# Rotary lanes moved by a VectorE shuffle instead of a TensorE product, and waits by column in a two-block fp32 layer

## The chip, the cores and the metric

One Trainium2 chip; the program runs on one of its cores. The metric is the device time of one execution in microseconds (us), median of the runs. All arithmetic is fp32. PE is TensorE, DVE VectorE, ACT ScalarE, POOL GpSimd, and SP the queue that issues the weight loads.

## What is computed

Two blocks for 256 tokens of width 1024. The first is a gated linear attention (GLA) with latent attention (MLA) beside it, an output product, a mixture of experts and a gated embedding:

```python
x = x + merged @ w_out[layer]
hm = rmsnorm(x, ln_moe[layer]).reshape(B * S, D)
x = x + hierarchical_moe(hm, ...)          # top-1 group of 8, then top-2 experts in it, 64 experts in all
ple_gate = jax.nn.sigmoid(rmsnorm(x, ln_ple[layer]) @ w_ple_gate[layer])
x = x + (p[layer] @ w_ple_proj[layer]) * ple_gate
```

The second is a modulated attention and convolution block; its queries and keys get a rotary embedding over rows and columns of a grid:

```python
def _rot_half_axial(u):
    u1, u2, u3, u4 = jnp.split(u, 4, axis=-1)          # head of 64: quarters of 16
    return jnp.concatenate([-u2, u1, -u4, u3], axis=-1)

def _apply_rope(u, cos, sin):
    return u * cos[None, :, None, :] + _rot_half_axial(u) * sin[None, :, None, :]

q = _apply_rope(_heads(parts[4]), cos, sin)
k = _apply_rope(_heads(parts[5]), cos, sin)
y_b = (silu(z_b) * attn) @ w_out_attn
y = (sigmoid(g_a) * y_a + sigmoid(g_b) * y_b) @ w_o
x = x + gt * rmsnorm(y, post_g)
```

## The kernel before

Each engine has one hand-written instruction stream, and semaphores tie the streams together. The order of the work is the order in which the streams are written.

**Weights.** SP streams weights in fills of 1 MB into a ring of 8 slots (`stream_a`, later line 535). A fill is issued once the product that used the slot has ended. In the experts' rounds 4 slots beside the ring join it, and a load waits for the count `moe_used`, which PE raises as it ends with the weights (lines 488 and 492 are the waits, seen in the trace as the line of the issue).

**Products.** A result is 256 output columns for all 256 tokens, in one PSUM bank. `product` (lines 555 to 573) runs two parts of 8 steps k over the width, 16 matmuls. With `feature` (L567) the weights are the stationary operand, without it (L570) the activations are. The profile records each fp32 matmul twice, so one product is 32 records. Banks 0 to 3 serve in turn (`bank_no`), banks 4 to 7 hold transposes and scores. Before the first matmul `product` waits for the bank and for the fill; whether the whole activation operand is there, the caller asks ahead of it.

**The operands.** `turn_rows` (L583) transposes an activation tile into banks 4 to 7. DVE (`turned`, L1524 or L1526) and ACT (L1045) copy the columns k into SBUF with a gain. For "ple" they take four columns each, for "two" (the operand of the second block's products) DVE takes all eight.

**The stages**, in PE's order: input products, modulation, MLA beside the gates, the GLA levels (L727, each masked into place by L1702, `diag` last), GLA values (L747), transposes (L753, L764) copied by ACT (L1200, L1210), products yb, ya, out, first context keys (kc) with router and ranks (L785 to L801), four embedding products (pp, L570), the gather of the first round (L826), and the expert rounds: up (L847), turn of the hidden rows (L874), down (L886), scatter (L919), whose four banks DVE adds to the residual X (L1868). Five context products (L859, L862) lie in rounds 1 and 2. Then ple, vc (last context values), the products zb, ga, gb, za, b, c, xin, q2, k2, v2, the attention (L981 to L1014), yattn, and last `wo` (L1027) in banks 0 to 7, followed by gain, squares, norm, residual and store.

**Rotation.** ACT copies each result of q2 and k2 to RAW (L1327). One product later PE multiplies RAW by the constant matrix `rot` (L959), into bank 4 or 5. DVE multiplies that bank by the sine (L1933) and RAW by the cosine (L1936), and adds (L1939, L1941). Between two rotations DVE does a quarter-step of the convolution (L1918 to L1923).

**Tail.** For each quarter of `wo`, DVE first writes the gained copy (L1992), then ACT squares the bank (L1359), DVE sums (L1997, L1998), POOL takes the power (L1489), DVE scales and adds X (L2005), SP stores (L540).

```python
pe.wait_ge(S("twoT"), 8)                              # before zb: all eight columns
pe.wait_ge(S("merged2"), 4)                           # before wo: all four pairs
act.wait_ge(S("y_gain"), 4 * t + n + 1)               # ACT's square behind DVE's gain
```

## Time and profile before

| | |
|---|---|
| runs before, us | 1294.29, 1291.46, 1290.39 |
| median | 1291.46 |
| profiled execution, its own time | 1288.38 |
| its span, first to last instruction | 1286.2 |
| PE busy | 1203.9 us, 94% of the span |
| DVE busy | 305.7 us, 24% |
| ACT busy | 211.1 us, 16% |
| POOL busy | 109.2 us, 8% |
| HBM traffic | 321.77 MB read, 251 GB/s over the span |

The profiled execution took 2.2 us more than its span, for what lies around the instructions. The 94% of PE say which engine is loaded, and they count as busy also the time in which its clock was lower. Where a stage waits has to be read from that stage.

### The profile page before, as it was taken

How to read it: one execution, taken by the hardware profiler on the slowest of the kernel's cores; microseconds unless marked ns; L12 is line 12 of the kernel's file. 1: busy time of each engine (PE TensorE's matmuls, PEld its weight loads, DVE VectorE, ACT ScalarE, POOL GpSimd, SP SyncE). 2: the span in 40 equal slices, each digit the busy share in tenths (PEclk: the TensorE clock that was granted, in tenths of full speed). 3: DMA queues.
4: the chain of work that ended last, by engine and by line, in shares of the span. 5: the costliest groups of instructions: out<-in, count | busy, mean ns of one | idle time of the engine just before them, and what ended most of it. 6: DMA issues, size and time to landing. Idle time of an engine off the chain costs nothing.

```text
span 1286.2 us, 14655 instructions
## 1 busy us (share of the span) xinstructions
PE 1203.9 (94%) x6053; PEld 833.1 (65%) x6053; DVE 305.7 (24%) x653; ACT 211.1 (16%) x433; POOL 109.2 (8%) x118
## 2 busy tenths in 40 slices
PE   6999998999999999998888889899999999999998
PEld 5887887887344445433232323788888888876687
DVE  1145348313111111110101010220001014526512
ACT  1232554103000000000000000210000000035501
POOL 0015045001000000000000000000000000125300
PEclk9999999999999999999999999899999999999999
DMA  9799322283699999999999999734444444443300
GB/s 320 258 291 325 124 77 93 76 360 135 271 406 411 411 411 416 415 419 416 420 416 420 416 418 384 231 120 164 144 150 164 146 149 138 151 144 124 99 1 33
DMA packets 149631, 323.60 MB, mean 252 GB/s; under 512 B 8671, under 2 KB 111562, under 8 KB 133194
## 3 DMA queue, kind: packets, MB, share of 16 engines
q1 hardware_dynamic: 143648, 315.33, 65.4%
q0 software_dynamic: 1536, 4.20, 1.2%
q10 hardware_dynamic: 4394, 3.31, 0.8%
q8 instruction: 40, 0.66, 0.2%
q14 instruction: 13, 0.11, 0.0%
HBM read 321.77 MB, written 1.05 MB: 251 GB/s over the span
## 4 chain that ended last, share of the span: by engine, by line
PE 82%; DMA 9%; ACT 2%; issue 2%; DVE 2%; SPq 1%; POOL 1%; ACTq 0%; DVEq 0%; POOLq 0%
PE bank L567 33%; PE bank L847 14%; PE bank L570 12%; DMA AR<-in_w 9%; PE bank L886 6%; PE bank L826 2%; PE bank L859 2%; PE bank L994 1%; PE bank L981 1%; PE bank L862 1%; PE bank L1027 1%; PE bank L1014 1%; PE bank L727 1%; PE bank L919 1%; PE bank L621 1%
## 5 line engine op out<-in xcount | busy, mean ns | idle before, releaser
L567 PE MATMUL bank<-HT,ring 128*128 128x256 f32 x1760 | 386.7, 380 | 3.0 <-DVE HT L1526 2.5
L567 PEld LDWEIGHTS bank<-HT,ring 128*128 128x128 f32 x1760 | 334.2, 191 | 51.2 <-issue 2.9
L847 PE MATMUL bank<-ring,AR 128*64 128x512 f32 x640 | 174.9, 606 | 20.0 <-DMA AR<-in_w 13.1
L847 PEld LDWEIGHTS bank<-ring,AR 128*64 128x64 f32 x640 | 55.4, 139 | 122.4 <-issue 121.8
L847 PE MATMUL bank<-AR 128*64 128x512 f32 x384 | 116.6, 605 | 2.4 <-DMA AR<-in_w 1.5
L886 PE MATMUL bank<-ring,AR 128*64 128x512 f32 x384 | 87.7, 598 | 11.4 <-ACT AR L1256 11.4
L570 PE MATMUL bank<-ring,HT 128*128 128x256 f32 (+1 forms) x384 | 81.9, 373 | 1.0 <-issue 1.0
L1853 DVE TENSOR_TENSOR AR<-AR,bank 128x256 f32<-128x256 f32 x32 | 13.5, 421 | 284.5 <-ACT AR L1247 283.7
L570 PEld LDWEIGHTS bank<-ring,HT 128*128 128x128 f32 x384 | 71.0, 190 | 11.1 <-issue 2.3
L570 PE MATMUL bank<-ring,AR 128*128 128x256 f32 x328 | 73.4, 386 | 3.4 <-DVE AR L1575 1.4
L1388 POOL TENSOR_TENSOR SM<-SM 128x2 f32<-128x2 f32 (+3 forms) x8 | 11.6, 1448 | 708.4 <-DVE SM L1506 658.2
L570 PEld LDWEIGHTS bank<-ring,AR 128*128 128x128 f32 x328 | 63.1, 194 | 13.0 <-DVE AR L1575 1.6
L1247 ACT ACTIVATE AR<-bank 128x256 f32<-128x256 f32 x32 | 12.3, 384 | 348.8 <-PE bank L847 348.8
L886 PEld LDWEIGHTS bank<-ring,AR 128*64 128x64 f32 x384 | 25.5, 136 | 58.1 <-issue 41.1
L847 PEld LDWEIGHTS bank<-AR 128*64 128x64 f32 x384 | 35.5, 139 | 40.0 <-issue 35.1
L567 PE MATMUL bank<-AR,ring 128*128 128x256 f32 x256 | 57.9, 383 | 1.0 <-ACT AR L1210 0.7
L567 PEld LDWEIGHTS bank<-AR,ring 128*128 128x128 f32 x256 | 47.8, 190 | 13.7 <-issue 6.1
L1868 DVE TENSOR_TENSOR X<-X,bank 128x512 f32<-128x512 f32 x32 | 19.8, 682 | 97.6 <-PE bank L919 97.6
L1566 DVE TENSOR_TENSOR AR<-AR,bank 128x512 f32<-128x512 f32 x12 | 8.2, 687 | 131.0 <-ACT AR L1317 80.1
L826 PEld LDWEIGHTS bank<-AR,HN 128*128 128x128 f32 x288 | 33.0, 192 | 6.3 <-issue 4.9
L826 PE MATMUL bank<-AR,HN 128*128 128x64 f32 x288 | 33.8, 276 | 1.0 <-ACT AR L1228 1.0
L886 PE MATMUL bank<-AR 128*64 128x512 f32 x128 | 29.2, 599 | 3.8 <-ACT AR L1256 3.8
(325 smaller groups left out, 1024.7 us busy)
## 6 DMA issues: line engine op xcount, KB each, us to landing
ring<-in_w SPq DMA_DIRECT2D x128, 1024.0 KB, 17.2
AR<-in_w SPq DMA_DIRECT2D x64, 1024.0 KB, 17.8
ring<-in_w_in SPq DMA_DIRECT2D x62, 1024.0 KB, 5.2
ring<-in_w_mod SPq DMA_DIRECT2D x12, 1024.0 KB, 5.9
AR<-in_w_in SPq DMA_DIRECT2D x5, 1024.0 KB, 17.0
ring<-in_w_out SPq DMA_DIRECT2D x4, 1024.0 KB, 5.1
ring<-in_w_ple_gate SPq DMA_DIRECT2D x4, 1024.0 KB, 9.5
ring<-in_w_out_conv SPq DMA_DIRECT2D x4, 1024.0 KB, 5.1
```

Of the source, the lines that this page charges most:

```text
L567: mm = pe.matmul(bank[:, part * T:part * T + T], w[:, k, c0 + part * P:c0 + part * P + P], act[:, k, :], start=(k == 0), stop=(k == k_n - 1))
L570: mm = pe.matmul(bank[:, part * 256:part * 256 + n], act[:, k, part * P:part * P + P], w[:, k, c0:c0 + n], start=(k == 0), stop=(k == k_n ...
L621: mm = pe.matmul(bank_of(i)[32 * g:32 * g + 32, 0:256], CC[:, k, :], w[:, k, :], start=(k < 4), stop=(k >= 4))
L727: mm = pe.matmul(bank[:, h * P:h * P + P], k[:, h, st * P:st * P + P], q[:, h, tt * P:tt * P + P], start=True, stop=True)
L826: mm = pe.matmul(B[0][:, k * SLOT:k * SLOT + SLOT], HN[:, t, k * P:k * P + P], SEL[:, t, 0:SLOT], start=(t == 0), stop=(t == TT - 1))
L847: mm = pe.matmul(bank[e * SLOT:e * SLOT + SLOT, :].rearrange("p (w n) -> p w n", w=2), XG[:, k, :], w, start=(k == 0), stop=(k == DK - 1))
L859: mm = pe.matmul(bank[:, part * T:part * T + T], w[:, k, part * P:part * P + P], HT[:, k, :], start=(k == 0), stop=(k == DK - 1))
L862: mm = pe.matmul(bank[:, part * 256:part * 256 + 256], HT[:, k, part * P:part * P + P], w[:, k, :], start=(k == 0), stop=(k == DK - 1))
L886: mm = pe.matmul(B[5][half * SLOT:half * SLOT + SLOT, :], HHT[:, p % 2, c, e * SLOT:e * SLOT + SLOT], w[:, c, half * 512:half * 512 + 512] ...
L919: mm = pe.matmul(B[SCATTER[2 * t + half]][:, :], STR[rows, t * P:t * P + P], YY[rows, :], start=True, stop=True)
L1853: V_.tensor_tensor(SGM[:, p % 2], SGM[:, p % 2], bank[:, 0:FE], ALU.mult).then_inc(S("moe_silu"), 1)
L1868: ins = V_.tensor_tensor(xs, xs, B[(0, 1, 2, 5)[2 * t + half]][:, :], ALU.add)
```

## The change

1. **Rotation.** The matmul with `rot` goes, and the matrix with it (128 of 1701 constant columns). DVE does a `stream_shuffle` of RAW within each group of 32 lanes, lane to (lane + 16) mod 32, then multiplies by a sine table that has the sign in it.
2. **Column waits.** `product` gets `ahead`, a wait before each k of the first part. It is used in the first product of yb, ya, out, ple, zb and yattn, and `wo` has the same. The producers raise their semaphores per column or pair. The `diag` level of GLA signals each half by itself.
3. **"two" operand.** Its columns 4 to 7 move from DVE to ACT.
4. **Around the first round.** Two steps k of kc run before the transposes of X. The fourth pp product moves behind the gather (banks 0, 1, 3, 2), and DVE computes the expert weights after the first selection of rows.
5. **Residual.** Scatter banks are (0, 1, 5, 2), DVE adds by half of the width, and the transposes after the last round start when the first half is in.
6. **Last product.** yattn uses banks 2, 3, 1, 0 and `wo` banks 4 to 7 first. ACT squares each bank before DVE writes the gained copy, and the norm of a row tile comes before its fourth gain.

```diff
-            def product(i, act, first=None, parts=(0, 1)):
+            def product(i, act, first=None, parts=(0, 1), ks=None, ahead=None):
...
                 for part in parts:
-                    for k in range(k_n):
+                    for k in ks or range(k_n):
+                        if ahead is not None and part == parts[0]:
+                            ahead(k)
...
+            def pairs_of(sem, base=0):
+                return lambda k: pe.wait_ge(S(sem), base + k // 2 + 1) if k % 2 == 0 else None
+            def two_engines(first, second):
+                return lambda k: pe.wait_ge(S(first if k < 4 else second), k % 4 + 1)
...
-            pe.wait_ge(S("gla_a"), len(LEVELS))
             for tt in range(TT):
+                pe.wait_ge(S("gla_a"), len(LEVELS) + tt)
...
-            products("yb", OTM)
+            products("yb", OTM, ahead=pairs_of("omT"))
...
-            products("ya", OTG)
+            products("ya", OTG, ahead=pairs_of("ogT"))
             turn_context(3, B[7])
-            pe.wait_ge(S("merged"), 4)
-            products("out", GATE[:, 0:8, :])
+            products("out", GATE[:, 0:8, :], ahead=pairs_of("merged"))
+            pe.wait_ge(S("cT"), 8)
+            product(of["kc"][0], HT, parts=(0,), ks=range(2))
             pe.wait_ge(S("emptied_dve"), emptied[of["out"][-1]][1])
-            pe.wait_ge(S("cT"), 8)
             turn_rows(lambda k, t: X[:, t, :].rearrange("p (q k) -> p k q", k=DK)[:, k, :])
-            product(of["kc"][0], HT, parts=(0,))
+            product(of["kc"][0], HT, parts=(0,), ks=range(2, DK))
...
             gather()
+            product(of["pp"][-1], PTR)
+            wait_emptied(of["pp"][2])
             moe_round(FIRST, first=True)
...
-            pe.wait_ge(S("moe_x"), rounds + 0)
-            turn_rows(cols(X))
-            pe.wait_ge(S("pleT_dve"), 4)
-            pe.wait_ge(S("pleT_act"), 4)
+            pe.wait_ge(S("moe_x"), rounds * 2)
+            turn_rows(cols(X), halfway=lambda: pe.wait_ge(S("moe_x"), rounds * 2 + 1))
             for i in of["ple"]:
-                product(i, PLT, first=True)
+                product(i, PLT, first=True, ahead=two_engines("pleT_dve", "pleT_act") if i == of["ple"][0] else None)
...
-            pe.wait_ge(S("twoT"), 8)
+            products("zb", HT, ahead=two_engines("twoT", "twoT_act"))
...
-                pe.matmul(B[4 + m % 2][:, :], const("rot"), RAW[:, m % 2, :], start=True, stop=True)\
-                  .then_inc(S("rot_ps"), 1)
...
-            pe.wait_ge(S("na_o"), H2 // 2)
-            products("yattn", HT)
-            pe.wait_ge(S("merged2"), 4)
+            products("yattn", HT, ahead=lambda k: pe.wait_ge(S("na_o"), k + 1))
...
+                        if t == n == 0:
+                            pairs_of("merged2")(k)
-                        mm = pe.matmul(B[4 * t + n][:, 0:256], GA[:, k, t * P:t * P + P], slot_view(f)[:, k, :],
+                        mm = pe.matmul(B[4 - 4 * t + n][:, 0:256], GA[:, k, t * P:t * P + P], slot_view(f)[:, k, :],
...
-                dve.wait_ge(S("rot_ps"), m + 1)
+                dve.wait_ge(S("emptied_act"), emptied[i][1])
                 d3 = dst.rearrange("p (a t) -> p a t", a=2)
-                V_.tensor_tensor(d3, B[4 + m % 2][:, :].rearrange("p (a t) -> p a t", a=2),
-                                 over(const("sinT").unsqueeze(1), 2, T), ALU.mult)
+                link(V_.stream_shuffle(dst, RAW[:, m % 2, :], [(lane + 16) % 32 for lane in range(32)]))
+                V_.tensor_tensor(d3, d3, over(const("sinT").unsqueeze(1), 2, T), ALU.mult)
...
-                    act.wait_ge(S("y_gain"), 4 * t + n + 1)
+                    act.wait_ge(S("wo_ps"), 4 * t + n + 1)
...
-                dve.wait_ge(S("wo_ps"), 4 * t + n + 1)
+                dve.wait_ge(S("y_sq"), 4 * t + n + 1)
```

How the streams move at three places. Lines of the changed file are 9 to 20 higher there: L576 and L579 are the two matmuls of `product`, L846 the gather, L867 the up product, L1036 the matmul of `wo`.

On PE, the last key products before:

```order
L959 MATMUL bank5<-AR,CST 128x512 [waits roped,emptied_act]
L567 MATMUL bank1<-HT,ring 128x256 [waits arr_a5,emptied_act]
L567 MATMUL bank1<-HT,ring 128x256 x15
L959 MATMUL bank4<-AR,CST 128x512 [waits roped,emptied_act]
L570 MATMUL bank2<-ring,HT 128x256 [waits arr_a6,emptied_act]
L570 MATMUL bank2<-ring,HT 128x256 x15
```

and now:

```order
L576 MATMUL bank1<-HT,ring 128x256 [waits arr_a5,emptied_act]
L576 MATMUL bank1<-HT,ring 128x256 x15
L579 MATMUL bank2<-ring,HT 128x256 [waits arr_a6,emptied_act]
L579 MATMUL bank2<-ring,HT 128x256 x15
L579 MATMUL bank3<-ring,HT 128x256 [waits arr_a7,emptied_act]
```

The rotation's matmul is gone from between the products, and no wait on `roped` is left there.

On DVE, one rotation (the first of the queries) as it is now, where the first row stands in place of nothing and the second took bank 4 before:

```order
L1949 STREAM_SHUFFLE AR<-AR 128x512 [waits emptied_act]
L1950 TENSOR_TENSOR AR<-AR,CST 128x512 [waits dve_chain]
L1952 TENSOR_TENSOR AR<-AR,CST 128x512
L1957 TENSOR_TENSOR AR<-AR 128x512 [waits dve_chain]
L1958 TENSOR_SCALAR AR<-AR 128x512 [waits dve_chain]
```

One instruction more for each of eight rotations; it waits for ACT's copy, no longer for PE.

On PE, from the third embedding product (pp) to the first expert product (up) before:

```order
L570 MATMUL bank2<-ring,AR 128x256 [waits emptied_dve]
L570 MATMUL bank2<-ring,AR 128x256 x3
L570 MATMUL bank3<-ring,AR 128x256 [waits emptied_act]
L570 MATMUL bank3<-ring,AR 128x256 x3
L826 MATMUL bank0<-AR,HN 128x64 [waits emptied_act,normed,sel]
L826 MATMUL bank0<-AR,HN 128x64 x15
L847 MATMUL bank3<-AR 64x512 [waits arr_m2,arr_m1,arr_m3,arr_m0,gath]
```

and now:

```order
L579 MATMUL bank3<-ring,AR 128x256 [waits emptied_act]
L579 MATMUL bank3<-ring,AR 128x256 x3
L846 MATMUL bank0<-AR,HN 128x64 [waits emptied_act,sel,normed]
L846 MATMUL bank0<-AR,HN 128x64 x15
L579 MATMUL bank2<-ring,AR 128x256 [waits emptied_dve]
L579 MATMUL bank2<-ring,AR 128x256 x3
L867 MATMUL bank3<-AR 64x512 [waits arr_m1,arr_m2,arr_m0,arr_m3,gath,emptied_act]
```

The last pp product stands between the gather and the product that needs what is gathered.

## Rows read from the trace of the kernel before

**Rows 1.** The page, the span in 40 slices: HBM traffic.
```profile
GB/s 320 258 291 325 124 77 93 76 360 135 271 406 411 411 411 416 415 419 416 420 416 420 416 418 384 231 120 164 144 150 164 146 149 138 151 144 124 99 1 33
```

**Rows 2.** Who PE waited for: line, releaser, us in total, times, longest.
```profile
PE bank L583 <- DVE X L1868: 2.6, 1, 2.6
PE bank L567 <- DVE HT L1526: 2.5, 1, 2.5
...
PE bank L1027 <- DVE AR L1989: 1.5, 1, 1.5
...
PE bank L747 <- DVE AR L1702: 1.4, 1, 1.4
...
PE bank L570 <- DVE AR L1753: 1.1, 1, 1.1
PE bank L826 <- ACT AR L1228: 1.0, 1, 1.0
...
PE bank L570 <- DVE AR L1524: 1.0, 1, 1.0
PE bank L847 <- DVE AR L1834: 0.8, 1, 0.8
PE bank L583 <- DVE X L1757: 0.8, 1, 0.8
...
PE bank L567 <- ACT AR L1210: 0.7, 1, 0.7
...
PE bank L567 <- DVE HT L1967: 0.5, 1, 0.5
PE bank L567 <- ACT AR L1200: 0.3, 1, 0.3
```

**Rows 3.** Windows (us, PE, PEld, DVE, ACT, POOL busy, PEclk, DMA share, GB/s) around the first rounds.
```profile
320.00:330.00 10.00, 10.00 (x50) 3.62 (x48) 1.62 (x6) 0.72 (x2) 0.00 (x0) 1.00 0.25 91
...
400.00:790.00 390.00, 354.64 (x1702) 151.64 (x1700) 45.82 (x110) 26.49 (x66) 0.00 (x0) 0.99 1.02 416
```

**Rows 4.** SP's issues (start, us, count), first round.
```profile
333.71 1.97 SPq L492 DMA_DIRECT2D ring<-in_w  x4
```

**Rows 5.** Timeline of the last GLA masks and of ACT's second operand copy.
```profile
224.74 1.32 DVE L1702 COPY_PREDICATED AR<-MSK,bank 128x512 f32<-128x512 uint8 x2 [0.45 <-PE bank L727]
...
247.00 1.09 ACT L1210 ACTIVATE AR<-bank 128x512 f32<-128x512 f32 x2 [12.27 <-PE bank L764]
```

**Rows 6.** Timeline after the last round: DVE's four columns of the "ple" operand.
```profile
809.18 1.65 DVE L1524 TENSOR_SCALAR AR<-bank,VEC 128x256 f32<-128x256 f32 x4
```

**Rows 7.** Windows after two idle times of PE, columns as in rows 3.
```profile
807.27:814.10 6.83, 5.85 (x22) 4.94 (x21) 1.73 (x5) 3.48 (x8) 0.69 (x1) 0.51 1.10 348
858.60:862.10 3.50, 3.50 (x9) 2.79 (x10) 0.00 (x0) 0.00 (x0) 0.00 (x0) 0.51 0.03 10
```

**Rows 8.** Timeline, DVE's eight columns of the "two" operand.
```profile
854.81 3.71 DVE L1526 TENSOR_SCALAR HT<-bank,SM 128x256 f32<-128x256 f32 x8 [8.40 <-PE bank L583]
```

**Rows 9.** Chain of work in order of time (start, us), rotation stage.
```profile
1075.49 0.86 PE bank L959 x2
1076.35 6.91 PE bank L567 x32
```

**Rows 10.** Windows of one query product with its rotation, and of three v2 products.
```profile
1075.33:1083.10 7.77, 7.77 (x36) 6.46 (x35) 4.12 (x8) 0.60 (x1) 0.00 (x0) 1.00 0.42 137
...
1122.98:1143.70 20.72, 20.68 (x96) 17.86 (x94) 2.63 (x3) 1.19 (x2) 2.12 (x3) 1.00 0.52 161
```

**Rows 11.** Timeline, one instruction on 128 x 512: product with sine, scaling.
```profile
1076.39 0.69 DVE L1933 TENSOR_TENSOR AR<-bank,CST 128x512 f32<-128x512 f32 x1 [3.47 <-PE bank L959]
...
1078.44 0.43 DVE L1942 TENSOR_SCALAR AR<-AR 128x512 f32<-128x512 f32 x1
```

**Rows 12.** Timeline, the tail after the last matmul.
```profile
1280.25 0.43 DVE L1992 TENSOR_TENSOR AR<-bank,PG 128x256 f32<-128x256 f32 x1 [3.03 <-PE bank L1027]
1280.71 0.38 ACT L1359 ACTIVATE HN<-bank 128x256 f32<-128x256 f32 x1 [2.98 <-DVE AR L1992]
```

More of the change, by code:

```diff
@@ L79, in constants @@
     put("ones", 1.0)
-    rot = np.zeros((P, P))
-    for r in range(P):
-        if (r % 32) < 16:
-            rot[r + 16, r] = -1.0
-        else:
-            rot[r - 16, r] = 1.0
-    put("rot", rot)
     half = HD // 2
@@ L802, in _ @@
             pe.wait_ge(S("pT"), 1)
-            products("pp", PTR)
+            for i in of["pp"][:-1]:
+                product(i, PTR)
             FIRST = 0
```

135 lines of the change are left out of this document (70 added, 65 removed).

## The prediction

> **What bounds the kernel now.** I read the span in slices first, then PE's waits, then the timeline around each wait that the change touches. PE is busy for 94% of the span, so the kernel is a chain of PE work, with one stretch of another kind. From the 12th to the 24th of the 40 slices (32.2 us each, so 354 to 772 us) HBM traffic stands at 406 to 420 GB/s [rows 1], and the window from 400 to 790 us shows the DMA engines full all the time while PE is busy for 355 of 390 us [rows 3]. There the experts' weights set the pace. Outside it a microsecond that PE waits or works is a microsecond of the end.
>
> Does a gain before the rounds reach the end, across a stretch bound by DMA? From 320 to 330 us the DMA engines are used at 0.25 [rows 3], so they start with no backlog. The burst that fills them is issued at 333.7 us, when PE has ended the second up product and freed its slots [rows 4]. An earlier PE therefore starts the full stretch earlier, with the same bytes behind it. I take it that the whole stretch moves by what is saved before it.
>
> **The change part by part.** First the waits before the rounds, each a line of [rows 2].
>
> GLA values (L747) wait 1.4 us for the last masks. The two masks start at 224.7 us, held until both halves of the scores are there, and take 0.66 us each [rows 5]. Now the first starts 0.4 us earlier, behind the mask of the level before, and PE starts after it instead of after the second: 0.4 + 0.66 = **1.1**. The second half of the values lies behind the first half's 16 records, longer than a mask, and waits for nothing. yb waits 0.3 for both copies and needs one: **0.3**. ya waits 0.7; its two copies take 1.09 [rows 5], so one of them, **0.5**, goes. out waits 1.1 for the fourth merged pair. Six steps k before it are 12 records of 0.216 us (6.91 by 32 [rows 9]), 2.6 us of cover: **1.1**. The transposes of X wait 0.8 for the residual. Four records of kc, 0.86 us, now lie in that gap, and 2.6 us of kc are left behind the transposes, which is still more than the 1.65 that DVE takes for four columns of such an operand [rows 6]: **0.7**. At the first round PE waits 1.0 before the gather for the last pp bank, and 0.8 before the up product for the gathered rows. The fourth pp product, 8 records or 1.7 us, now covers the second wait, and the first has lost its cause. The expert weights leave DVE's path to the selection: **1.8**. Sum before the rounds: **5.5**.
>
> In the rounds the scatter banks change places and DVE adds in another order. The next round's first use of these banks lies behind an up product. If that cover were lost, each round would show its adds, up to the 2.6 us that PE waits for them after the last one [rows 2], but nothing in the change takes it away: 0.
>
> After the last round the transposes wait 2.6 for the residual [rows 2]. They can start half an addition stage sooner, about 1.2 us, but ACT's squares still need all of X, and DVE's columns stand behind them. So I count nothing for that. The first ple product waits until all four DVE columns are there. These take 1.65 us [rows 6], and now one column suffices, 0.4 us: **1.2**.
>
> At the operand "two" DVE does eight columns in 3.71 us [rows 8] and PE waits 2.5. Now PE can start with the first column as its own transposes end, since DVE makes a column in 0.46 us, PE uses one in 0.43, and ACT makes the other four beside it. The wait of **2.5** goes. There is more in it. After this wait the granted clock is 0.51 for 3.5 us [rows 7], the lower of the two levels, 1.2 GHz instead of 2.4. That cost 3.5 x 0.49 = **1.7**, which goes with the wait. After the last round it stands at 0.51 for 6.8 us too. Before it PE had stood still for 2.6 us; now it would stand still for 1.3 and, after the transposes, for nearly 2. I let that loss stay.
>
> The rotation is the largest term. A product with its rotation matmul takes 7.77 us, without it 6.91, and the matmul has 0.86 in the chain [rows 9, 10]. Eight of them: **6.9**. DVE gets a shuffle of 128 x 512 for each. The trace before has no shuffle. Its bounds are 0.43, the cheapest pass over 128 x 512 with one source, and 0.69, the one with two [rows 11]; I take 0.6, since a shuffle has one source but permutes it. DVE is busy 4.12 us per product [rows 10], and would be 4.8 of 6.91. At either bound it stays hidden, and behind the last key product lie four v2 products, 27.6 us. If the cover were gone, the eight shuffles would cost 4.8. The Trainium skill (VectorE: DVE Perf Modes, the perf-mode tier table) gives a shuffle one rate only, some 2400 ns for 2048 elements. By that an estimate for 512 is 0.6 us, and the sum stays the same.
>
> yattn waits **0.5** for the last head pair, which it now needs at its eighth step. wo waits **1.5** for the last merged pair [rows 2], now needed 2.6 us after its start. In the tail ACT's square stands behind DVE's 0.43 us gain [rows 12]. Now it comes first, and the gain lies beside POOL's power: **0.5**.
>
> **Sum:** 5.5 + 1.2 + 4.2 + 6.9 + 2.0 + 0.5 = **20.3 us**. The profiled execution took 1288.4, so 1268.1 by its own time. The median of the runs is 3.1 above it, and the forecast goes by the median: 1291.5 - 20.3 = **1271.2**.
>
> **The rivals.**
>
> *The rounds swallow what comes before them.* If the full DMA stretch ended at its old time, 5.5 would be lost: gain 14.8, **1276.7**. For it speaks the traffic of over 400 GB/s in 13 slices [rows 1]. Against it speaks that its start hangs on PE [rows 3, 4]. Chance 0.10.
>
> *Column waits cost PE its flow.* The change adds 29 waits between matmuls (1 in yb, 1 in ya, 3 in out, 7 each in ple, zb and yattn, 3 in wo). A weight load takes 0.19 us (17.86 by 94 [rows 10]) and is otherwise hidden beside a matmul. If each wait laid one bare, that is 5.5: gain 14.8, again **1276.7**. Against it: three v2 products in a row, each with two waits at its start, take 20.72 us, exactly three times 6.91 [rows 9, 10], so a wait that is already met costs nothing. For it: in the first ple product the waits are not met in advance. The Trainium skill (TensorE: Matmul & The Clock Gate, the spec table) says that TensorE pulls weight loads ahead of matmuls in flight. A load held at a wait could not be pulled, and then the sum would be this rival's. Chance 0.10.
>
> *The clock stays up after the last round too.* Idle is cut in two pieces there. If no fall follows, the first ple product loses nothing to it. It ran at the lower level from 811.1 to 814.1 [rows 7], 3.0 x 0.5 = 1.5 more: **1269.7**. It falls after idle times of 2.5 and 2.6 us in [rows 2], and new pieces are each shorter, but little work lies between them. Chance 0.12.
>
> *The shuffle is slow, and DVE becomes the bound.* This is the one that ends slower. From the first query result to the end of v2, 11 products or 76 us pass. DVE needs 33 of them without the shuffles [rows 10]. Up to (76 - 33) / 8 = 5.3 us per shuffle nothing shows. Above it every microsecond costs eight, the gain is gone at 5.3 + 20.3 / 8 = 7.9, and at 9 us each the kernel would be 8 x (9 - 7.9) = 9 slower than before, **1300**. That is 13 times the dearer of the two bounds. Chance 0.02.
>
> *Half of the column waits do nothing*, since some other condition of the same product comes late, a bank or a fill. The rotation (6.9) and the two operand (4.2) would stay, with 2 to 4 of the rest: gain about 14, **1277**. The views show no such second wait that is late at these places. Chance 0.04.
>
> **How the numbers follow.** Forecast 0.60, the clock 0.12, rounds 0.10, flow 0.10, half 0.04, shuffle 0.02, and 0.02 for what I have not thought of. The likeliest case by itself spans 1269 to 1273. The range reaches to 1266.5, which is the clock case with 3 us for the spread of the runs and for gains that I left at zero, and to 1278, which holds the cases at 1277. What a measurement of this kernel can tell from no change is 0.3%, 3.9 us. All cases but the last two lie well beyond it on the faster side: faster 0.96. The last two share same 0.02 and slower 0.02.
>
> **What would show it.** In the profile after: no gap between key products, 6.91 us each; STREAM_SHUFFLE near 0.6 us; PE's wait of 2.5 before zb gone and the clock at full level there; the first up product 5.5 us earlier, and the last scatter by the same amount. If the last scatter moves by less, the rounds rival holds. If the first products of ple, zb or yattn take longer than their neighbours at full clock, the flow rival holds. A DVE that is busy throughout a key product would prove the shuffle rival. The forecast is wrong in its size if the clock falls at other places than before.

## The result, and the profile after

| | before | changed |
|---|---|---|
| median of the runs, us | 1290.93 (4 runs, 1288.43 to 1294.29) | 1266.53 (4 runs, 1264.93 to 1270.90) |
| ratio | | 0.9832, 95% interval 0.9810 to 0.9854 |
| profiled execution, us | 1288.38 | 1264.93 |
| its span | 1286.2 | 1263.1 |

The ratio is 21.7 us less, between 18.8 and 24.5. The forecast was 1271.2 with a range of 1266.5 to 1278.0: faster, as forecast, with the median 0.03 us inside the range's lower end. The sum made against the profile was 20.3 us; the two profiled executions differ by 23.1 in span. The forecast is 4.7 above the median. Of that, 3.1 is the sum, against 23.4 between the two executions by their own times. 0.5 is the median of before, 1290.93 with a fourth run where I had 1291.46. 1.0 is the spread of the runs: the profiled execution lies 2.6 below its median before and 1.6 below it after.

The page of the changed kernel, busy time of the engines:

```profile
PE 1190.9 (94%) x6037; PEld 824.5 (65%) x6037; DVE 310.9 (25%) x665; ACT 212.7 (17%) x437; POOL 110.6 (9%) x118
```

PE is busy for 13.0 us less, of which 6.9 is the rotation's matmuls. Most of the rest, 5.1, is lower clock that went (below). The other part of the gain, 10 us, is waiting that went, and the share of 94% hides it, since both numbers shrank.

Who PE waited for, as in [rows 2] (line, releaser, us in total, times, longest):

```profile
PE bank L747 <- DVE AR L1698: 5.5, 4, 2.6
PE bank L579 <- DVE AR L1538: 1.8, 1, 1.8
...
PE bank L603 <- DVE X L1873: 1.4, 1, 1.4
...
PE bank L768 <- DVE AR L1718: 0.8, 1, 0.8
PE bank L1023 <- DVE AR L1977: 0.8, 1, 0.8
...
PE bank L576 <- ACT AR L1219: 0.3, 1, 0.3
```

Of the waits in [rows 2] that the change touches, the one before zb (2.5), before wo (1.5), before out (1.1), those around the first round (1.0 and 0.8), before the transposes of X (0.8), before yattn (0.5) and before yb (0.3) are gone. Three are smaller: ya 0.3, GLA values 0.8, and the transposes after the last round 1.4 instead of 2.6. The first ple product waits 1.8 where it waited 1.0, because its transposes end earlier and the columns have not moved as much. The first line, 5.5 us in four waits, is of the GLA score levels, where before has 4.5 in three. A score product at 196 us took 1.6 us less in this execution, and 1.0 of that turned into waiting (more on it below).

The chain of work (start, us, what), from ple to v2; the rows of before are [rows 9] and those named in the prediction:

```profile
803.62 41.68 PE bank L579 x192
...
847.05 248.64 PE bank L576 x1152
1095.69 27.64 PE bank L579 x128
```

The 1152 records from zb to the end of the key products are one unbroken piece: 36 products of 6.91 us, with no rotation between them and no slow start.

The rotation on DVE, by its line (us from first to last start, then the form), and the window of one query product, columns as in [rows 3]:

```profile
L1949 DVE LOAD_MASK_SELECT AR<-AR x8: 14/14/14, 1048.0 to 1096.4; - x8
L1949 DVE STREAM_SHUFFLE AR<-AR x8: 721/724/727, 1048.0 to 1096.4; 128x512 f32<-128x512 f32 x8
```
```profile
1068.50:1075.41 6.91, 6.91 (x33) 6.08 (x33) 4.85 (x10) 0.60 (x2) 0.00 (x0) 1.00 0.45 152
```

A shuffle takes 0.724 us where I took 0.6, just above the dearer of my two bounds. DVE is busy 4.85 of 6.91 us (before 4.12 of 7.77 [rows 10]).

The windows of [rows 3] and [rows 7], moved to the same places of this execution:

```profile
393.86:783.86 390.00, 355.57 (x1702) 151.24 (x1700) 45.85 (x110) 26.41 (x66) 0.00 (x0) 0.98 1.02 416
799.50:806.50 7.00, 5.07 (x29) 4.29 (x30) 2.90 (x7) 3.64 (x8) 0.70 (x1) 1.00 1.10 348
847.05:850.55 3.50, 3.50 (x17) 3.07 (x17) 0.63 (x2) 1.53 (x4) 0.00 (x0) 1.00 0.76 263
```

The DMA stretch is the same, with the same 416 GB/s and as many records. After the last round and at the start of zb the granted clock is 1.00 where it was 0.51 [rows 7].

The start of each stage in the two profiles, and by how much it is earlier, gives the account by stage:

| start of | before | changed | earlier by | this step | forecast |
|---|---|---|---|---|---|
| last two GLA score levels | 220.95 | 220.41 | 0.54 | 0.5 | 0 |
| GLA values | 226.12 | 224.98 | 1.1 | 0.6 | 1.1 |
| ya (after yb) | 248.14 | 246.17 | 2.0 | 0.8 | 0.8 |
| out | 263.73 | 260.66 | 3.1 | 1.1 | 1.1 |
| router | 297.90 | 293.72 | 4.2 | 1.1 | 0.7 |
| first up product | 318.87 | 312.73 | 6.1 | 2.0 | 1.8 |
| last scatter | 802.33 | 796.15 | 6.2 | 0.0 | 0 |
| ple | 811.08 | 803.62 | 7.5 | 1.3 | 1.2 |
| zb | 858.58 | 847.05 | 11.5 | 4.1 | 2.5 |
| v2 | 1115.18 | 1095.69 | 19.5 | 8.0 | 7.7 |
| attention | 1144.44 | 1124.10 | 20.3 | 0.9 | 0.9 |
| yattn | 1222.92 | 1202.15 | 20.8 | 0.4 | 0.5 |
| wo | 1252.32 | 1229.97 | 22.4 | 1.6 | 1.5 |
| end | 1286.2 | 1263.1 | 23.1 | 0.7 | 0.5 |

(The forecast's 6.9 for the rotation is split: seven of the eight lie before v2, one behind it; its 1.7 for the clock is in the v2 row.) Four rows differ from the forecast by over 0.3 us: the two of the GLA stage, the router and zb.

### The profile page after: what moved, and what is told of

It reads as the page before. It is cut to its first block, busy times and chain, and to the rows that moved or that the text cites. A ratio compares the mean times of both kernels' runs of the same rounds, so it can differ in the third digit from the quotient of the medians.

```text
span 1263.1 us, 14644 instructions
## 1 busy us (share of the span) xinstructions
PE 1190.9 (94%) x6037; PEld 824.5 (65%) x6037; DVE 310.9 (25%) x665; ACT 212.7 (17%) x437; POOL 110.6 (9%) x118
## 4 chain that ended last, share of the span: by engine, by line
PE 86%; DMA 6%; ACT 2%; issue 2%; DVE 1%; POOL 1%; ACTq 0%; SPq 0%; DVEq 0%; POOLq 0%
PE bank L576 34%; PE bank L867 16%; PE bank L579 12%; PE bank L906 8%; DMA AR<-in_w 6%; PE bank L846 3%; PE bank L879 2%; PE bank L944 1%; PE bank L1003 1%; PE bank L990 1%; PE bank L882 1%; PE bank L1023 1%; PE bank L1036 1%; PE bank L747 1%; PE bank L641 1%
## 5 line engine op out<-in xcount | busy, mean ns | idle before, releaser
L576 PE MATMUL bank<-HT,ring 128*128 128x256 f32 x1760 | 384.0, 379 | 0.0
L576 PEld LDWEIGHTS bank<-HT,ring 128*128 128x128 f32 x1760 | 332.8, 190 | 44.7 <-issue 0.4
L867 PE MATMUL bank<-ring,AR 128*64 128x512 f32 x640 | 176.0, 605 | 20.5 <-DMA AR<-in_w 14.9
L867 PEld LDWEIGHTS bank<-ring,AR 128*64 128x64 f32 x640 | 55.6, 139 | 124.4 <-issue 123.8
L867 PE MATMUL bank<-AR 128*64 128x512 f32 x384 | 119.4, 613 | 0.3 <-issue 0.3
L579 PE MATMUL bank<-ring,HT 128*128 128x256 f32 (+1 forms) x384 | 81.8, 373 | 1.0 <-issue 1.0
L579 PEld LDWEIGHTS bank<-ring,HT 128*128 128x128 f32 x384 | 71.0, 190 | 10.2 <-issue 1.3
L579 PE MATMUL bank<-ring,AR 128*128 128x256 f32 x328 | 71.9, 380 | 3.2 <-DVE AR L1538 1.8
L579 PEld LDWEIGHTS bank<-ring,AR 128*128 128x128 f32 x328 | 61.9, 190 | 11.8 <-issue 2.0
L867 PEld LDWEIGHTS bank<-AR 128*64 128x64 f32 x384 | 36.2, 140 | 37.9 <-issue 36.4
L576 PE MATMUL bank<-AR,ring 128*128 128x256 f32 x256 | 57.9, 383 | 0.3 <-ACT AR L1219 0.3
L576 PEld LDWEIGHTS bank<-AR,ring 128*128 128x128 f32 x256 | 47.8, 190 | 12.8 <-issue 6.6
L846 PEld LDWEIGHTS bank<-AR,HN 128*128 128x128 f32 x288 | 33.1, 192 | 5.0 <-issue 4.9
L846 PE MATMUL bank<-AR,HN 128*128 128x64 f32 x288 | 33.8, 275 | 0.0
L906 PE MATMUL bank<-AR 128*64 128x512 f32 x128 | 29.2, 598 | 3.8 <-ACT AR L1265 3.8
```

What stands on the lines that cost most here:

```text
L576: mm = pe.matmul(bank[:, part * T:part * T + T], w[:, k, c0 + part * P:c0 + part * P + P], act[:, k, :], start=(k == 0), stop=(k == k_n - 1))
L579: mm = pe.matmul(bank[:, part * 256:part * 256 + n], act[:, k, part * P:part * P + P], w[:, k, c0:c0 + n], start=(k == 0), stop=(k == k_n ...
L846: mm = pe.matmul(B[0][:, k * SLOT:k * SLOT + SLOT], HN[:, t, k * P:k * P + P], SEL[:, t, 0:SLOT], start=(t == 0), stop=(t == TT - 1))
L867: mm = pe.matmul(bank[e * SLOT:e * SLOT + SLOT, :].rearrange("p (w n) -> p w n", w=2), XG[:, k, :], w, start=(k == 0), stop=(k == DK - 1))
L906: mm = pe.matmul(B[5][half * SLOT:half * SLOT + SLOT, :], HHT[:, p % 2, c, e * SLOT:e * SLOT + SLOT], w[:, c, half * 512:half * 512 + 512] ...
```

## The experiments

Twelve kernels ran, on three occasions; each time the kernel before ran beside them (medians 1288.4, 1287.8 and 1288.8 us). I compare by the ratio to before, and places by their distance from a landmark of the same execution, since executions of one instruction stream differ at their start: the first 64 records of the input products take 11.49 us in eight of the 14 profiles (both kernels' among them) and 13.20 to 13.83 us in the other six. The last section says what the traces show of it.

### The rotation, undone and alone

Undone in the changed kernel (the matrix with both signs positive, the sign stays in the sine table):

```diff
-            products("q2", HT)
-            products("k2", HT)
-            products("v2", HT)
...
+            for m, i in enumerate(of["q2"] + of["k2"]):
+                product(i, HT)
+                if m:
+                    rotate(m - 1)
+            product(of["v2"][0], HT)
+            rotate(7)
...
-                dve.wait_ge(S("emptied_act"), emptied[i][1])
+                dve.wait_ge(S("rot_ps"), m + 1)
...
-                link(V_.stream_shuffle(dst, RAW[:, m % 2, :], [(lane + 16) % 32 for lane in range(32)]))
-                V_.tensor_tensor(d3, d3, over(const("sinT").unsqueeze(1), 2, T), ALU.mult)
+                V_.tensor_tensor(d3, B[4 + m % 2][:, :].rearrange("p (a t) -> p a t", a=2),
+                                 over(const("sinT").unsqueeze(1), 2, T), ALU.mult)
```

Expected: 

> The changed kernel with the eight rotation matmuls back on TensorE and the shuffles gone; all column waits and reorderings stay. My theory, that terms on TensorE's chain simply add: 8 x 0.86 = 6.9 us more than the changed kernel (about 1273.4 against 1266.5), and 17 to 18 us less than before. Rival, that the rotation was half hidden by something else: less than 4 us more. The profile should show 7.77 us from one query product to the next, and all other stages at the same distances as in the changed kernel.

Measured: 1273.49 us (1272.41 to 1274.92), ratio 0.9887 (0.9870 to 0.9903), so 14.6 us of gain are left. Its chain in the key products:

```profile
1056.92 0.86 PE bank L988 x2
1057.78 6.91 PE bank L583 x32
1064.69 0.86 PE bank L988 x2
1065.55 6.91 PE bank L583 x32
```

The 0.86 is back behind every product, as in [rows 9].

The other way round, the kernel before with the shuffle alone; waits, orders and banks stay as they were. The edit is the one above with its signs turned; the matrix goes, and the sine table is that of the changed kernel.

Expected: 

> The kernel before with the rotation by shuffle alone; all waits, orders and banks as before. Theory, the terms add: 8 x 0.86 = 6.9 us less than the kernel before, near 1281, ratio 0.9947, and the stage from the start of the first zb product to the first v2 product is shorter by the 7 rotations in it, 6.0 us. Rival, part of the gain hangs on the rest of the change (DVE's queue is late without it): less than 5 us. TensorE's waits of 2.5 and 2.6 us stay, and the clock falls after both.

Measured: 1280.34 us (1279.24 to 1284.00), ratio 0.9935 (0.9921 to 0.9950), 8.4 us less with an interval of 6.4 to 10.2. In its chain zb to the last key product:

```profile
811.85 41.68 PE bank L563 x192
857.76 250.59 PE bank L560 x1152
1108.36 27.64 PE bank L563 x128
```

From zb to v2 are 250.6 us, before 256.6 (1115.18 - 858.58): 6.0 less, as seven rotations of 0.86 should give. The 250.59 against 248.64 is the slow start of zb, which this kernel still has. The gain by rotation alone (8.4) and all but the rotation (14.6) add up to 23.0, beside 21.7 for both together, within the intervals. The rotation's term holds, and it needs nothing from the rest of the change. The clock fell after both waits, but differently than in the profile before: after the last round it is low in the transposes alone (3.56 us, 2.29 at full clock), and the first ple product shows nothing of it.

### What a wait costs that is already met

```diff
                         if ahead is not None and part == parts[0]:
                             ahead(k)
+                        else:
+                            pe.wait_ge(S("early_in"), EARLY)
```

Some 1320 waits on a count reached long before, one ahead of nearly every matmul of every product (the trace has 2728 records of such matmuls, two for each, and 40 matmuls have a wait of the change already).

Expected: 

> The changed kernel with a wait that has long been met in front of each of some 1340 matmuls in the products (a semaphore of the input loads). My theory, that a met wait costs TensorE nothing: within 2 us of the changed kernel. Flow rival, that each wait lays a weight load of 0.19 us bare: about 250 us more. Anything between gives the price per wait: 13 us would be 10 ns each, and then the 29 waits of the change cost 0.3 us.

Measured: 1267.67 us (1266.47 to 1269.30), ratio 0.9841 (0.9825 to 0.9858), where the changed kernel had 0.9832 and, run again, 0.9828 (below). The chain:

```profile
807.65 41.68 PE bank L581 x192
851.08 248.64 PE bank L578 x1152
```

Both pieces take to the hundredth what they take without the waits. The flow rival priced 29 waits at 5.5 us, 0.19 each; 1320 of that price would be 250 us. It is refuted for waits that are met. For the change's own waits, which are not all met in advance, the comparison is with the rotation alone above, which has none of them: its 192 records from ple on also take 41.68 us. The 192 records of the changed kernel take no longer for the waits between them. The Trainium skill (TensorE: Matmul & The Clock Gate, the spec table) has weight loads pulled ahead of matmuls in flight, and by that rule each wait could have bared one. The chain shows no such cost here.

### The operand "two", back on DVE

```diff
-                nc.scalar.activation(HT[:, k, :], B[4 + k // 2][:, (k % 2) * T:(k % 2) * T + T], ACT.Identity,
-                                     scale=ACOL[:, 0, k:k + 1], bias=MODT[:, k, 0:1]).then_inc(S("twoT_act"), 1)
...
-            turned("two", "twoT", lambda k: ACOL[:, 0, k:k + 1], bias=lambda k: MODT[:, k, 0:1])
+            turned("two", "twoT", lambda k: ACOL[:, 0, k:k + 1], range(DK), lambda k: MODT[:, k, 0:1])
...
-            products("zb", HT, ahead=two_engines("twoT", "twoT_act"))
+            pe.wait_ge(S("twoT"), 8)
+            products("zb", HT)
```

Expected: 

> The changed kernel with the operand of the second block's products made as before: VectorE all eight columns, TensorE waits for all. My theory: 2.5 us of wait come back, and with them the fall of the granted clock for about 3.5 us, 1.7 us: 4.2 us more than the changed kernel. Rival, that the clock after this wait has nothing to do with it: 2.5 us more, clock at 1.00 right after the wait.

Measured: 1269.47 us (1267.42 to 1272.49), ratio 0.9853 (0.9836 to 0.9871). By the ratios that is 2.7 us more than the changed kernel, less than the wait and the clock together (2.5 + 1.95), but the two intervals overlap. A clock that does not fall in every execution would give less, too; one profile cannot tell. The trace shows the term in one execution. The wait, and the stage's timeline (start, us, engine, line, what, idle before):

```profile
PE bank L576 <- DVE HT L1536: 2.5, 1, 2.5
```
```profile
848.15 1.91 PE L603 MATMUL bank<-CST,HN 128*128 128x128 f32 x16
...
848.79 3.71 DVE L1536 TENSOR_SCALAR HT<-bank,SM 128x256 f32<-128x256 f32 x8 [8.39 <-PE bank L603]
852.56 4.76 PE L576 MATMUL bank<-HT,ring 128*128 128x256 f32 x13 [2.50 <-DVE HT L1536]
```

Both come back as in [rows 8]: the wait of 2.5, and behind it thirteen records in 4.76 us, where fifteen take 3.40 in the changed kernel. In the chain the 1152 records take 250.59 instead of 248.64, so the clock after this wait is worth 1.95 us. With the wait, the term is 4.4 in this profile, forecast 4.2.

### Work put in front of the rounds

48 matmuls whose result nobody reads, ahead of the gather of the first round:

```diff
+            for n in range(48):
+                pe.matmul(B[7][:, 0:256], HT[:, n % DK, 0:P], HT[:, n % DK, :], start=True, stop=True)
             pe.wait_ge(S("normed"), nth("hm", NORMED))
```

Expected: 

> The changed kernel with 48 extra matmuls of 128 x 256 (96 records of 0.216 us, 20.7 us in all) on TensorE just before the gather of the first round; their result is not used. My theory, that the stretch bound by DMA starts when TensorE frees the first slots and moves as a whole: 20.7 us more. Rival, that the DMA stretch has slack in front and swallows what comes before: clearly less, 0 to 10 us more. The last scatter should be later by the same amount as the first up product.

Measured: 1287.93 us (1285.66 to 1289.84, 10 runs), ratio 0.9997 (0.9987 to 1.0007): the whole gain of the change is eaten. In its chain the added work, 20.72 us:

```profile
309.71 20.72 PE bank L949 x96
```

From the first up product (335.73) to the last scatter (820.48) this execution takes 484.75 us; before it was 483.46 and in the changed kernel 483.42. The other experiments lie between 482.3 and 485.4. So 20.7 us put ahead of a stretch of 400 us in which the DMA engines are full pass through it whole, to about 1.4. The rounds do not swallow what comes before them. As [rows 4] suggested, their fills start when PE frees their slots: four fills are issued at 350.5 us here and at 327.5 in the changed kernel, each time as the second up product ends.

### More shuffles, to find the cover's edge

```diff
-                link(V_.stream_shuffle(dst, RAW[:, m % 2, :], [(lane + 16) % 32 for lane in range(32)]))
+                for _ in range(6):
+                    link(V_.stream_shuffle(dst, RAW[:, m % 2, :], [(lane + 16) % 32 for lane in range(32)]))
```

and the same with 12. Expected with six: 

> The changed kernel with each of the eight shuffles done six times over (one took 0.72 us, six take 4.5 us); the result is the same. My theory, that VectorE has 5.3 to 5.6 us of cover for each rotation, counted through the v2 products: no more than 1 us over the changed kernel, though VectorE then works 8.7 us per query product of 6.9. Rival, that the cover is only the rest of the one product, 2.0 us: 8 x (3.7 - 2.0) = 14 us more.

Expected with twelve: 

> The same with twelve, 8.9 us for each rotation. My theory: cover runs out at about 5.5 us, so 8 x (8.9 - 5.5) = 27 us more than the changed kernel, which is slower than before. Rival, cover of 2.0 us: 8 x (8.2 - 2.0) = 50 us more.

Measured with six: 1266.76 us (1265.97 to 1268.10), ratio 0.9835 (0.9819 to 0.9851). One product's window (columns as in [rows 3]):

```profile
1061.50:1068.41 6.91, 6.91 (x34) 6.08 (x33) 6.57 (x16) 0.60 (x1) 0.00 (x0) 1.00 0.45 144
```

DVE is busy 6.57 of 6.91 us and PE does not notice. Zb to v2 is still 248.64 us. Five more shuffles, 3.8 us for each rotation, cost nothing, since v2 covers what DVE has left over.

Measured with twelve: 1296.73 us (1295.85 to 1298.46), ratio 1.0074 (1.0058 to 1.0091), 30 us more than the changed kernel. A window that holds one turn of DVE (13.4 us from one rotation to the next) and two products of PE, and PE's timeline:

```profile
1062.40:1076.60 14.20, 14.20 (x67) 12.52 (x66) 13.52 (x35) 1.17 (x2) 0.00 (x0) 1.00 0.45 149
```
```profile
1114.80 10.02 PE L579 MATMUL bank<-ring,HT 128*128 128x256 f32 x32 [4.11 <-ACT AR L1341]
1127.75 8.68 PE L579 MATMUL bank<-ring,HT 128*128 128x256 f32 x32 [2.93 <-ACT AR L1341]
1152.93 3.78 PE L990 MATMUL bank<-AR 64*128 64x512 f32 x8 [16.50 <-DVE AR L1956]
```

DVE is now the bound. The queries still do not feel it, though ACT's copies (L1341) fall behind. The first to pay are the v2 products, which wait 4.1 and 2.9 us for banks that ACT cannot empty while DVE holds RAW, and then the attention, which waits 16.5 for the last rotation. After each of these idle times PE is slow: 10.02 and 8.68 us for a product of 6.91. From zb to the attention it is 304.7 us, in the changed kernel 277.1: 27.6 more. Most of what is left of the 30 lies behind it, where the attention starts at a granted clock of 0.51 (1152.9 to 1158.2 us). The prediction's formula for the slow shuffle gives, for 12 x 0.765 = 9.2 us each, 8 x (9.2 - 5.3) = 31. It is right in form, and 3 us too dear. By the measured 27.6 the edge lies near 9.2 - 27.6 / 8 = 5.7 us for a rotation's shuffles, or seven of them. This is an estimate, since nothing between six and twelve was run.

### Parts of the path after the last round

First, the transposes wait for the whole residual, as before:

```diff
-            pe.wait_ge(S("moe_x"), rounds * 2)
-            turn_rows(cols(X), halfway=lambda: pe.wait_ge(S("moe_x"), rounds * 2 + 1))
+            pe.wait_ge(S("moe_x"), rounds * 2 + 1)
+            turn_rows(cols(X))
```

Expected: 

> The changed kernel, but the transposes after the last round wait for both halves of the residual as before, which makes TensorE's idle time 2.6 us instead of 1.4 there. In the profiles so far the clock after the last round fell in three executions (before, rotation back, operand two back) and stayed up in three. Theory A, that the split of the residual is worth nothing in time: same start of the first ple product, 7.5 us after the last scatter, and at most the 1.6 us of a clock fall in some executions, so 0 to 1.6 us more. Theory B, that the split keeps the clock up: the fall is there in the profile and 1.6 us show in the median.

Measured: 1267.70 us (1264.28 to 1269.50), ratio 0.9840 (0.9820 to 0.9861): no difference that the runs can tell. The timeline from the last scatter on:

```profile
802.98 3.32 PE L603 MATMUL bank<-CST,X 128*128 128x128 f32 x16 [2.58 <-DVE X L1873]
...
805.26 1.65 DVE L1538 TENSOR_SCALAR AR<-bank,VEC 128x256 f32<-128x256 f32 x4
```

PE waits 2.6 again, and the transposes take 3.32 us instead of 2.29. Ple starts 7.9 us after the last scatter (798.41), in the changed kernel 7.5 after its own (796.15). This 0.4 goes with the clock and not with the wait. DVE's columns are held by ACT's squares, as the text said: they start at 805.26, behind the mean that follows the squares, 6.85 us after the last scatter, and 6.85 it is in the changed kernel, too. What holds ple back here are the transposes, which end at 806.30. In 2.29 us they would have ended at 805.27, as the first column starts, and ple would have followed 7.5 us after the scatter (an estimate from these rows). What the split may do is move the fall of the clock: with the whole residual it begins in the transposes in all three profiles, and where it falls with the split, it does so about the start of ple. That this gains anything is not shown. From the last scatter to the end of the 192 records it is 49.6 us here, 49.2 in the changed kernel, and 50.8 in those profiles of the split in which the clock fell in ple.

So I took that hold away. Second, the operand's columns ahead of the squares on ACT, and ahead of the mean on DVE. They read the transposes alone, and the norm comes in later:

```diff
-            sumsq(X, "ple")
             turned("ple", "pleT_act", lambda k: vec("ln_ple", k), PLT)
+            sumsq(X, "ple")
...
-            mean_sq("ple", D)
             turned("ple", "pleT_dve", lambda k: vec("ln_ple", k), dst=PLT)
+            mean_sq("ple", D)
```

Expected: 

> The changed kernel with the gained columns of the ple operand made before the squares and the mean on ScalarE and VectorE, since the norm is needed only when the first ple product has ended. TensorE's wait of 1.8 us before ple should go, as the first columns can follow the transposes: 1.8 us less than the changed kernel, and up to 1.6 more where the clock no longer falls, 1.8 to 3.4 us less. Rival, that the columns are held by the transposes or that the squares now come too late for the first sigmoid: no gain, and a new wait of TensorE on a ple bank.

Measured: 1263.58 us (1262.90 to 1263.87), ratio 0.9811 (0.9795 to 0.9827). The timeline of the changed kernel, and then of this one:

```profile
799.53 2.29 PE L603 MATMUL bank<-CST,X 128*128 128x128 f32 x16 [1.39 <-DVE X L1873]
...
803.00 1.65 DVE L1538 TENSOR_SCALAR AR<-bank,VEC 128x256 f32<-128x256 f32 x4
...
803.62 8.66 PE L579 MATMUL bank<-ring,AR 128*128 128x256 f32 x39 [1.81 <-DVE AR L1538]
```
```profile
801.76 1.66 DVE L1538 TENSOR_SCALAR AR<-bank,VEC 128x256 f32<-128x256 f32 x4 [0.21 <-DVE X L1873]
802.36 1.57 ACT L1054 ACTIVATE AR<-bank,VEC 128x256 f32<-128x256 f32 x4 [5.38 <-PE bank L603]
802.43 3.75 PEld L579 LDWEIGHTS bank<-ring,AR 128*128 128x128 f32 x18
802.53 3.83 PE L579 MATMUL bank<-ring,AR 128*128 128x256 f32 x17
```

The wait of 1.8 is gone. DVE's first column comes right behind the residual, and ple starts behind its transposes, in the chain 5.7 us after the last scatter (797.03 to 802.70) instead of 7.5. The squares end 3.3 us into ple (806.00), and nobody is waiting for them. The intervals of this run and of the changed kernel overlap; the comparison on one chip follows below.

### The open 0.45 us at the GLA masks

In the changed kernel the first diag mask still starts 0.45 us after the mask before it, though its half of the scores is there earlier. I let it wait for the same half of the level before alone:

```diff
-                if n:
+                if n and lv != "diag":
                     dve.wait_ge(S("gla_a"), n)
...
+                    if lv == "diag":
+                        dve.wait_ge(S("gla_a" if st else "gla_half"), n if st else 1)
...
+                    elif lv == "base_bwd":
+                        ins.then_inc(S("gla_half"), 1)
```

Expected: 

> The changed kernel, in which the first diag mask waits for the first mask of the level before (the same half of the tile) instead of for both. Nothing else moves. Open point: in the changed kernel the first diag mask still starts 0.45 us after the end of the mask before it, though half of the scores has been there for half a microsecond. Theory A, it waits for VectorE's own count of the level before, and what takes 0.45 is the way from the end of a mask to its own semaphore: the 0.45 goes, the mask starts right behind the one before it, and the values start 4.1 us after the last scores' start instead of 4.57. Theory B, it waits for TensorE's signal of the first half, which comes later than the records show: 0.45 and 4.57 stay. The time of the whole is within 0.5 us of the changed kernel in both.

Measured: 1265.89 us (1263.87 to 1268.43), ratio 0.9818 (0.9802 to 0.9834). The timeline of the changed kernel, then of this one:

```profile
222.39 1.36 DVE L1718 COPY_PREDICATED AR<-MSK,bank 128x512 f32<-128x512 uint8 x2 [0.96 <-PE bank L747]
...
224.20 1.33 DVE L1718 COPY_PREDICATED AR<-MSK,bank 128x512 f32<-128x512 uint8 x2 [0.45 <-PE bank L747]
224.98 3.20 PEld L768 LDWEIGHTS bank<-AR 128*128 128x128 f32 x28 [1.03 <-DVE AR L1718]
```
```profile
222.47 2.59 DVE L1720 COPY_PREDICATED AR<-MSK,bank 128x512 f32<-128x512 uint8 x4 [0.96 <-PE bank L747]
...
224.50 3.84 PE L768 MATMUL bank<-AR 128*128 128x128 f32 x32 [0.28 <-DVE AR L1720]
```

The four masks are one piece now, 2.59 us, and the values start 4.0 us after the scores' start (220.49) instead of 4.6. So the 0.45 was DVE's wait for its own count of the level before, which the profile puts down to PE. Why such a wait takes 0.45 here, and only 0.04 between two shuffles that wait for each other in the same way, was not tried. For the time of the whole the effect is too small to tell.

### Both edits, and the changed kernel again beside them

Expected of the changed kernel with the columns first and the half chain: 

> The changed kernel with two edits: the columns of the embedding operand ahead of the squares on ScalarE and ahead of the mean on VectorE (as in the run with the columns first), and the first diag mask behind its own half only. Theory, both gains stand on the path and add up: about 1.7 + 0.45 us less than the changed kernel run beside it, near 1264. Rival, the earlier gain is lost in the rounds' DMA stretch, or the clock falls elsewhere: within 1 us of the changed kernel. The wait of 1.8 before the first embedding product is gone in either case.

Expected of the changed kernel once more: 

> The changed kernel once more, on the chip of the three others and between the same runs of the kernel before. Theory: 1266.5 to 1267.5, ratio 0.982 to 0.984. It also shows whether the clock stays up after the last round in a second execution (first embedding and context products together 41.7 us) or falls (43.3). If it falls here, the changed kernel has both outcomes, and my likeliest case and its rival differ only by which execution is looked at.

| | median, us | lowest to highest | ratio to before (95%) |
|---|---|---|---|
| changed kernel again | 1266.41 | 1264.31 to 1270.65 | 0.9828 (0.9809 to 0.9846) |
| both edits | 1262.56 | 1261.86 to 1262.98 | 0.9792 (0.9779 to 0.9805) |

The two edits beat both kernels: 26.8 us less than before, and 3.8 less than the changed kernel on the same chip; the slowest run of the one is faster than the fastest of the other. The theory gave 1264, from gains of 1.7 and 0.45, so 1.5 more came than it had. The runs of both edits lie within 1.2 us of each other and those of the columns first within 1.0, while the changed kernel spreads over 6. One part of it may be the clock after the last round, which costs 1.6 in some executions of the changed kernel, while in both profiles with the columns first it stays up (41.44 us for the 192 records). The clock at 196 us (below) differs between executions as well. That does not account for 6 us, and what the rest is stays open. In its second profile the changed kernel has the clock up, too (41.68 us).

## Why the prediction was right, point by point

**The bound.** Right. PE's chain sets the end outside the rounds, and what is saved ahead of the DMA stretch arrives behind it: 6.14 us at the first up product, 6.18 at the last scatter, and the added 20.7 of work likewise. The rounds rival falls.

**Before the rounds, 5.5.** It became 6.1 in the profile. Besides the half chain, no run undoes one of these parts by itself; they rest on the waits that are gone and on the table of stages. The step on the GLA values failed: "Now the first starts 0.4 us earlier, behind the mask of the level before". It stood behind DVE's own semaphore, not behind the second half of the scores, and the term is 0.6, not 1.1. I had taken the name of the releaser in [rows 5] at its word. yb, ya and out came as worked out. The router's row has 1.1 for 0.7, of which 0.3 lies in the out products (27.63 us instead of 27.91) and only the rest at the transposes. 0.5 came from a place that I had no term for: at 196 us, a score product of 16 records takes 3.62 us in the profile before and 2.05 in the changed one, at a granted clock of 0.66 and 1.00 from 196 to 201 us. The change moves no instruction there, and it is not an effect of the change: the changed kernel's second profile has 3.67 us and 0.66 there, like before.

**After the last round, 1.2.** Measured 1.3, and all of it is the column waits. Before, ple starts 1.9 us after DVE's first column (809.18 to 811.08), now 0.6 after it (803.00 to 803.62), and the first column itself comes 6.85 us after the last scatter in both. "So I count nothing for that" held for the idle time.

**The clock after the last round.** Here a rival came true in the profile: "I let that loss stay", and it went. The 192 records from ple on take 41.68 us instead of 43.26, 1.6 for the 1.5 that the rival gave. But this is not a property of the changed kernel. Of the profiles that have the changed order up to here, the clock fell in four (rotation back, "two" back, six and twelve shuffles: 43.3 or 43.4 us), and stayed in five (the changed kernel twice, the met waits, the front work, the half chain: 41.68). A chance of 0.12 for one outcome and of 0.60 for the other was the mistake, and that the fall was absent from this profile is luck. With idle of 1.4 and 1.8 us and 2.3 us of work between, both occur about as often.

**The operand "two", 4.2.** Measured 4.4, by the profile after and by undoing it: 2.5 of wait and 1.95 of clock. The clock's part was sized as the 3.5 us of the window in [rows 7] at 0.51. That window does hold the whole low stretch (the clock stands at 0.93 from 862.0 to 862.5 us), so the other 0.25 is not low clock that was left out. A part of it is the first record, which the second follows after 0.53 us, while the others at the lower level come every 0.43; the rest stays open.

**The rotation, 6.9.** Right to a tenth by the chain, and within their intervals by undoing it and by doing it alone. The shuffle is dearer than I took it (0.72 for 0.6), which costs nothing. The Trainium skill (VectorE: DVE Perf Modes, the perf-mode tier table) gave the same 0.6 as an estimate, by scaling its one figure to 512 elements, 0.12 too low here. The cover was worth far more than the difference: six shuffles in place of one are free. The slow-shuffle rival was a true mechanism with its edge at 5.3 for about 5.7, and nothing to drive it.

**Column waits.** Each place shows its gain in the table, and a met wait costs nothing that can be measured. Both rivals on them fall.

**yattn, wo and the tail, 2.5.** Measured 2.8. In the tail ACT's last square starts as the last matmul ends, and DVE's gain lies beside POOL's power:

```profile
1257.63 0.38 ACT L1373 ACTIVATE HN<-bank 128x256 f32<-128x256 f32 x1 [2.98 <-PE bank L1036]
...
1258.40 0.41 DVE L2008 TENSOR_TENSOR AR<-bank,PG 128x256 f32<-128x256 f32 x1
1258.57 0.56 POOL L1503 TENSOR_TENSOR SM<-SM 128x1 f32<-128x1 f32 x1 [13.25 <-DVE SM L2014]
```

**Together.** 20.3 by the terms, minus 0.5 at the GLA masks, plus 0.4 at the router, 0.2 at the first round, 0.1 after the last round, 0.3 more of clock at "two", 0.3 at yattn, wo and the end, makes 21.1 for what the change does. 1.6 and 0.5 of clock that happened to stay up in this execution bring it to 23.2, and the spans differ by 23.1. The ratio of the runs says 21.7. So the terms and their mechanisms hold, but that the median lies inside the range is partly luck: the margin is 0.03 us, and the changed kernel run again has 1266.41.

## What to carry to other kernels

Where an operand is made in pieces, let its first consumer wait for each piece: in these runs a wait of PE that is met cost nothing, and each unmet one avoided saved itself and sometimes the clock behind it. Before ordering an engine's work, ask which of its outputs PE needs next. Squares for a norm that is applied later must not stand ahead of the columns. And when the engine that the profile names as releaser had been done for some time, look for a wait of the engine on its own count.

## What the runs showed of the hardware

A fall of the granted clock is not settled by the instruction stream. After a single idle time of 2.5 us before zb it fell in each of the three profiles that have that wait (before, "two" back, rotation alone). After 2.6 us before the transposes it fell in all three (before, whole residual, rotation alone); in two of them it was back when ple began, or soon after, and in the third not until some 3 us into ple. After the 2.6 us before the score product at 196 to 199 us, which all 14 profiles have, it fell in five (before, changed again, rotation alone, six shuffles, whole residual). After two idle times of 1.4 and 1.8 us it fell in four of nine.

The first 64 records take 11.49 us in eight profiles and 13.20 to 13.83 us in six, and the windows show a granted clock of 1.00 over them in all. Their pace says otherwise. With six shuffles they follow each other every 0.427 us until 20.5 us, the pace of zb's first records at a granted clock of 0.50, where the changed kernel has 0.216 from the start. The trace's own records of the clock begin at 20.5 us there, and at 19.4 to 20.1 in the other five; in the eight they begin at 14.3 to 15.6, before these matmuls. For the time before its first record a window shows 1.00. So at the start the clock has to be read from the pace of the records.

Two kernels that differ by 2 us in one profile each may thus be the same, and a stage's length has to be compared in more than one execution.

A shuffle of 128 x 512 fp32 takes 0.72 us, with 14 ns for loading its mask, about as long as a product of two such tiles takes on DVE (0.69 [rows 11]). Twelve of them in a row follow each other every 0.765 us, each waiting for the one before it.
